# A two-layer diffusion step on one core: the passage to the second layer, the router and the weight units of the expert loop reordered

## The reference

```python
def _swiglu(h, wg, wu, wd):
    return (jax.nn.silu(h @ wg) * (h @ wu)) @ wd

def _moe(h, w_router, wg, wu, wd):
    ...
    logits = (t @ w_router).astype(jnp.float32)
    top_v, top_i = lax.top_k(logits, TOP_K)
    top_w = jax.nn.softmax(top_v, -1)
    ...
    for e in range(N_EXPERTS):
        y = y + gates[:, e:e + 1] * _swiglu(t, wg[e], wu[e], wd[e])

def _layer(x, cond, lp, ffn, latent, ctx_k, ctx_v, s0):
    mod = jax.nn.silu(cond) @ lp['w_mod'] + lp['b_mod']
    sh1, sc1, g1, sh2, sc2, g2 = jnp.split(mod[:, None, :], 6, -1)
    h = x * (1 + sc1) + sh1
    mix, kb, vb, s = _mixer(h, lp, latent, ctx_k, ctx_v, s0)
    x = _ln(DN_ALPHA * x + g1 * mix, lp['ln_g'][0], lp['ln_b'][0])
    h = x * (1 + sc2) + sh2
    x = _ln(DN_ALPHA * x + g2 * ffn(h), lp['ln_g'][1], lp['ln_b'][1])
```

## Time and profile before

| | us |
|---|---|
| median of 3 runs | 1976.18 (1976.16 to 1976.51) |
| the profiled execution | 1976.08, of which the span is 1973.8 |
| PE busy | 1883.9 (95%) |
| DVE busy | 1401.5 (71%) |
| ACT busy | 1088.6 (55%) |
| last down matmul of the dense stage ends, about | 566.5 |
| first matmul of cva in layer 1 | 608.76 |
| gather for the first expert begins | 932.14 |
| one pass of the expert loop | 125.32 |

### The profile page before, as it was taken

One profiled execution on the slowest core, in us unless ns is written; L12 is line 12 of the kernel. 1 busy time (PEld: TensorE's weight loads), 2 busy tenths in 40 slices (PEclk: granted clock), 3 DMA queues, 4 the chain that ended last, 5 costly groups with the idle time before them and its releaser, 6 DMA issues.

```text
span 1973.8 us, 23686 instructions
## 1 busy us (share of the span) xinstructions
PE 1883.9 (95%) x9097; PEld 1416.1 (72%) x9097; DVE 1401.5 (71%) x1424; ACT 1088.6 (55%) x1025; POOL 29.8 (2%) x53
## 2 busy tenths in 40 slices
PE   4999999999979999998999999999999999999995
PEld 2885554677858855545788888888888888888884
DVE  2576853644564858525788888988889888888886
ACT  2443332444434533313777767777777777777773
POOL 1000010000000000100000000000000000000000
PEclk9999999999989999998999999999999999999997
DMA  9765344576573553434799999999999999999993
GB/s 353 254 228 205 128 157 147 196 255 213 193 262 140 201 213 139 136 126 150 272 367 341 354 337 358 364 341 356 354 341 363 342 357 362 333 366 341 352 368 110
DMA packets 228430, 531.69 MB, mean 269 GB/s; under 512 B 5128, under 2 KB 7744, under 8 KB 228368
## 3 DMA queue, kind: packets, MB, share of 16 engines
q1 hardware_dynamic: 161728, 369.77, 52.2%
q10 hardware_dynamic: 63472, 151.27, 21.0%
q0 software_dynamic: 3168, 9.80, 1.6%
HBM read 528.20 MB, written 2.62 MB: 269 GB/s over the span
## 4 chain that ended last, share of the span: by engine, by line
PE 94%; DVE 2%; ACT 2%; issue 1%; DMA 1%; ACTq 0%; POOL 0%; DVEq 0%; POOLq 0%
PE ps L856 20%; PE ps L857 20%; PE ps L858 20%; PE ps L786 16%; PE ps L843 2%; PE ps L807 2%; PE ps L809 2%; PE ps L810 2%; PE ps L1240 2%; PE ps L820 2%; PE ps L1268 1%; PE ps L1118 1%; DMA arena<-in_cv_w 1%; PE ps L971 0%; PE ps L1002 0%
## 5 line engine op out<-in xcount | busy, mean ns | idle before, releaser
L2274 DVE TENSOR_TENSOR arena_r<-ring,arena_r 128x2048 fp32r<-128x2048 f32 x224 | 512.0, 2292 | 107.8 <-ACT arena_r L1410 103.4
L1410 ACT ACTIVATE arena_r<-ring 128x2048 fp32r<-128x2048 f32 x224 | 428.9, 1915 | 85.1 <-PE ps L858 85.0
L856 PE MATMUL ps<-arena_r 128*128 128x512 f32 x1128 | 449.3, 398 | 24.2 <-DVE arena_r L1776 14.5
L857 PE MATMUL ps<-arena_r 128*128 128x512 f32 x1128 | 443.2, 393 | 0.0
L858 PE MATMUL ps<-arena_r 128*128 128x512 f32 x1128 | 413.0, 392 | 0.0
L2274 DVE TENSOR_TENSOR ring_r<-ring,ring_r 128x2048 fp32r<-128x2048 f32 x113 | 258.9, 2291 | 37.5 <-ACT ring_r L1410 35.9
L856 PEld LDWEIGHTS ps<-arena_r 128*128 128x128 f32 x1128 | 214.4, 190 | 71.5 <-issue 20.1
L858 PEld LDWEIGHTS ps<-arena_r 128*128 128x128 f32 x1128 | 214.2, 190 | 46.4
L857 PEld LDWEIGHTS ps<-arena_r 128*128 128x128 f32 x1128 | 214.6, 190 | 44.0
L1410 ACT ACTIVATE ring_r<-ring 128x2048 fp32r<-128x2048 f32 x113 | 216.7, 1917 | 50.0 <-PE ps L858 49.8
L856 PE MATMUL ps<-ring_r,arena_r 128*128 128x512 f32 (+1 forms) x592 | 235.2, 397 | 0.7 <-issue 0.7
(11 more groups left out here) (236 smaller groups left out, 1918.6 us busy)
## 6 DMA issues: line engine op xcount, KB each, us to landing
ring<-in_moe_w_gate SPq DMA_DIRECT2D x57, 2048.0 KB, 7.8
ring<-in_moe_w_up ACTq DMA_DIRECT2D x48, 2048.0 KB, 7.8
ring<-in_moe_w_down SPq DMA_DIRECT2D x32, 2048.0 KB, 7.8
ring<-in_w_in SPq DMA_DIRECT2D x28, 2048.0 KB, 8.4
ring<-in_w_mod SPq DMA_DIRECT2D x24, 2048.0 KB, 8.6
ring<-in_moe_w_down ACTq DMA_DIRECT2D x24, 2048.0 KB, 7.8
ring<-in_moe_w_up SPq DMA_DIRECT2D x8, 2048.0 KB, 7.9
ring<-in_ffd_w_gate SPq DMA_DIRECT2D x5, 2048.0 KB, 13.9
```

What stands on the lines that cost most here:

```text
L856: mm(o_, hi, w_hi[:, n], start=start, stop=False)
L857: mm(o_, hi, w_lo[:, n], start=False, stop=False)
L1410: act_(e_part(j)[0], raw_part(j), ACT.Copy).then_inc(part_hi, 1)
L2274: V.tensor_tensor(w_lo, raw_part(j), w_hi.bitcast(F32), ALU.subtract).then_inc(part_lo, 1)
```

## The change

Four things are done at once.

1. **Passage.** Layer 1's modulations 4 and 5 move from the passage into layer 1's mixer, where layer 0 has them; the turning of modulation 3 moves into the dense stage. The last four down parts (from `DAPART` = 18) run first for group 0 and then for group 1. All four weight parts of layer 1's v are cast before the norms, two of them in buffers of their own, and the modulation's columns are gathered before them as well. PE turns x of both groups before v; ACT modulates both halves of group 0. The slots of the ring shift by one from there on.
2. **Mixers.** The turnings of `kbtok` and `kctxT` stand before the gate matmul `mgate(5, 1)`, and ACT's copies before the silu. Modulation 11 stands before the wait for mT.
3. **Router.** ACT's exponential stands before the last two gate copies and the first cast, and the casts of parts 0 and 1 both stand before the loop; in the loop ACT runs one part further ahead.
4. **Expert loop.** A gate and up unit now holds 512 rows of 512 gate columns and 512 up columns; G and U of one width are summed up over four parts, side by side in two banks. Every unit is loaded by two transfers of 1 MB, all from SP's queue. The turning of the width before stands after the second of the four parts, the scattering after the first two parts of the pass, and the bank table is new.

PE's order in the passage, before: the end of the down matmuls (L856 to L858 with `ring_r`), modulation (L843 with `condT`), turnings (L820; `x` is the normalised x, `arena` a modulation row).

The diff, cut to its core:

```diff
-        if l:
-            modT(l, 3), mod(l, 4)
         for g in range(G):
             p("hT", l, g, 0), p("hT", l, g, 1)
-            if l and g == 0:
-                modT(l, 4), mod(l, 5), modT(l, 5)
+        for g in range(G):
             p("v", l, g)
...
+DAPART = FF_D // P - 4
...
-EUNITS = []
-for _i in range(EC):
-    EUNITS += [("g", _i), ("u", _i)]
+EUNITS = [("gu", _i, _h) for _i in range(EC) for _h in range(2)]
...
+            if phase_of(j) == "mixer1":
+                b = (20992, 18432, 0, 2048)[s] if j - PHASE["mixer1"] < DPARTS else (15360, 17408, 0, 2048)[s]
+            else:
+                b = (0, 2048, 15360, 17408)[s]
...
+                halves = [(dst[:, :, 512 * h:512 * h + 512],
+                           a[w][0, e, rows_, 512 * name[1]:512 * name[1] + 512].rearrange("(c p) n -> p c n", p=P))
+                          for h, w in enumerate(("moe_w_gate", "moe_w_up"))]
             eng.wait_ge(part_lo, E * EQ + (PART_BASE + 2 * (i - XRING + 1)))
-            dst = slot(i % XRING).rearrange("p (c n) -> p c n", c=4 if name[0] == "d" else 8)
-            eng.dma_start(dst, e_source(name, e)).then_inc(w_loaded[i % XRING], 16)
+            for to, src in halves:
+                eng.dma_start(to, src).then_inc(w_loaded[i % XRING], 16)
...
+                turned(("kbtok", l), [kbT[:, j * T:j * T + P] for j in range(4)])
+                pe.wait_ge(ctx_in, 16 * (l + 1))
+                turned(("kctxT", l), [kctx[:, j * P:(j + 1) * P] for j in range(4)])
                 mgate(5, 1)
...
+                mod_mm(l, 11)
                 for g in range(G):
                     copied("mT", l, g, 0), copied("mT", l, g, 1)
-                mod_mm(l, 11)
...
+                    for g in range(G):
+                        for f in range(DAPART, FF_D // P):
+                            dense_down(f, [g])
...
+                        gu = [(e_claim(p, E, "G", i), 0), (e_claim(p, E, "U", i), 512)]
+                        for q in range(4):
...
+                                inss = split_mm([(o_, slice(D * c + n, D * c + n + 512)) for o_, n in gu], hg_hi[:, ks], hg_lo[:, ks],
+                                                w_hi, w_lo, k == 0, k == KD - 1)
...
+                            if q == 1 and i:
+                                turn(i - 1)
...
+                    st.next(gate_arg)
+                    act_(route[:, 100:102], route[:, 98:100], ACT.Exp).then_inc(gate_exp, 1)
+                gate_row(1)
...
+                    v1 = DFIRST["v", 1]
+                    early_hi(v1), early_hi(v1 + 1)
+                    act_(stat[:, 54:55], ident[:, 0:1], ACT.Sqrt)
+                    early_hi(v1 + 2)
                     norm_sqrt(1)
+                    early_hi(v1 + 3)
                 else:
-                    expert_high(0, 0, 0)
-                    st.next(gate_arg)
-                    act_(route[:, 100:102], route[:, 98:100], ACT.Exp).then_inc(gate_exp, 1)
+                    expert_high(0, 0, 0), expert_high(0, 0, 1)
...
-                    for j in range(1, EQ + 1):
-                        if (j + 3) % 2 == 0 and (j + 3) // 2 in ACT_UNITS:
-                            load_expert_unit(sc, E, e, (j + 3) // 2)
+                    for j in range(2, EQ + 2):
...
+                    early_lo(DFIRST["v", 1]), early_lo(DFIRST["v", 1] + 1)
+                    mod_columns(0, 4, 8, 1, modT[:, 96:192].rearrange("p (c g) -> p c g", g=G), 64)
                     dv.wait_ge(ln_in, 32 * 2)
```

More of the change, by code:

```diff
@@ L193, in plan @@
         p("oT", l, 1)
+        p("kbtok", l), p("kctxT", l)
         mg(l, 5, 1)
         p("cvT", l, 0), p("cvT", l, 1)
-        p("kbtok", l), p("kctxT", l), p("bias", l, 0), p("bias", l, 1)
+        p("bias", l, 0), p("bias", l, 1)
         for i in range(4):
@@ L351 @@
             EUSED.append(USED_PER)
-ACT_UNITS = range(EPARTS, len(EUNITS), 2)
 HI_PER = 4 + EC
@@ L1073, in _ @@
                     turned(("cvT", l, g), [acc[:, g * 512 + j * P:g * 512 + (j + 1) * P] for j in range(4)])
-                turned(("kbtok", l), [kbT[:, j * T:j * T + P] for j in range(4)])
-                pe.wait_ge(ctx_in, 16 * (l + 1))
-                turned(("kctxT", l), [kctx[:, j * P:(j + 1) * P] for j in range(4)])
                 pe.wait_ge(bias_in, 64 * (l + 1))
@@ L1415, in _, with modulated @@
             for l in range(DEPTH):
-                def modulated(kind, sh, scl, g):
-                    await_product(sc, kind, l, g, 1)
-                    for j in range(4):
-                        k = 4 + j
-                        ins = act_(hT[:, k * T + g * P:k * T + (g + 1) * P], bank((kind, l, g, 1))[:, j * P:(j + 1) * P],
-                                   ACT.Identity, bias=modcol(l, sh + k, g), scale=modcol(l, scl + k, g))
-                    free(ins, kind, l, g, 1)
+                def modulated(kind, sh, scl, g, halves=(1,)):
+                    for h in halves:
+                        await_product(sc, kind, l, g, h)
+                        for j in range(4):
+                            k = 4 * h + j
+                            ins = act_(hT[:, k * T + g * P:k * T + (g + 1) * P], bank((kind, l, g, h))[:, j * P:(j + 1) * P],
+                                       ACT.Identity, bias=modcol(l, sh + k, g), scale=modcol(l, scl + k, g))
+                        free(ins, kind, l, g, h)
                 def norm_sqrt(n):
@@ L1442, in _ @@
                 else:
[L1443 to L1447 removed]
+                    modulated("hT", 0, 8, 0, range(2))
+                    high_h("hT", l, 0)
+                    norm_sqrt(1)
+                    modulated("hT", 0, 8, 1)
+                    high_h("hT", l, 1)
                 hi_unit("cva")
@@ L1551, in _ @@
                 gla_turned(1)
+                take(kbtok, ("kbtok", l))
+                take(kctxT, ("kctxT", l))
                 mgate(5, 1)
@@ L1561, in _ @@
                     free(ins, "cvT", l, g)
-                take(kbtok, ("kbtok", l))
-                take(kctxT, ("kctxT", l))
                 softmax_exp(Pm)
```

220 lines of the change are left out of this document (97 added, 123 removed).

## The result

The changed kernel takes 1942.04 us (median of 4 runs, 1941.47 to 1942.18), the kernel before 1976.17; the ratio is 0.9822, 95% interval 0.9811 to 0.9834. The profiled execution took 1941.47 us with a span of 1939.2, against 1976.08 and 1973.8: 34.6 us less. The forecast was 1944, range 1937 to 1953.

The account below looks back on a forecast made before the run. PE, on the chain of waits for 94% of the span, was taken as the bound, so gains lie at seams where it waits. Passage -11.9, keys -8.0, modulation 11 -3.8, router -8.5 sum to -32.2: 1976.1 to 1943.9, say 1944, range 1937 to 1953.

Parts of the forecast that it names:

- passage with modulation 3's turning: Dense stage to layer 1's cva: 42.2 us shrinks to 24.8, -17.4; modulation 3's turning moved to the dense stage, +0.5.
- modulations 4 and 5 in layer 1's mixer: Layer 1's mixer, cva to rope: taking these modulations lengthens it from 75.33 to layer 0's 80.35 us, +5.0.
- turning of cached keys, twice: Before attention scores in each mixer: copies ahead of silu remove PE's 2.41 us idle, 9.48 to 4.0 us; -8.0 together.
- modulation 11, twice: Each mixer: its eight matmuls fill PE's 1.92 us wait for ACT's copies of mT; -3.8 together.
- router, parts 0 and 1, loop: Router and first expert: exponential 3.4 us earlier, part 1 cast during the gather, -8.5 (bounds -9.5 and -4); loop 0.
- last link: Passage: low part of h, on DVE after group 1's norm, ends at 11.1 us; v of group 0 starts about 11.75.
- nine of v's matmuls at half clock: Passage, v of group 0: 9 of 24 matmuls at 0.427 us and 15 at 0.233, together 7.3 us.
- the rule of the Trainium skill: Passage: transposes do not count as work for the clock, so v stays slow about four more matmuls, 0.8 us; not counted.
- A: Expert loop: loads become the bound; gain gone at 0.19 us over per unit, 1991 us at 6.25 us; chance 0.08.
- B: Expert loop: ACT or DVE late at parts 4 and 8, PE waits twice an expert, 5 to 8 us; chance 0.12.
- C: Passage yields half: v of group 0 waits for something placed too early, -6 instead of -11.9, 1950 us; chance 0.08.
- D: Router not earlier: parts 0 and 1 at half clock or table load on gate copies, -4, 1948 us; chance 0.05.

## Why the prediction was right

| term | forecast | measured |
|---|---|---|
| passage with modulation 3's turning | -16.9 | -18.0 |
| modulations 4 and 5 in layer 1's mixer | +5.0 | +4.9 |
| turning of cached keys, twice | -8.0 | -8.5 |
| modulation 11, twice | -3.8 | -3.6 |
| router, parts 0 and 1, loop | -8.5 | -9.9 |
| start of the kernel | 0 | +0.5 |
| sum | -32.2 | -34.6 |

The passage, the keys, the mixer and the router gave more than forecast, modulation 11 and the start a little less: the forecast of 1944 was 2 us too high.

**Passage.** The chain was right in its first links: group 0's norm under the down matmuls, then DVE's norm of group 1 with PE idle for 6.40 us. Its last link was another one. The sum lets v wait for the low part of h and adds 0.65 us for which it names no row; it leaves out PE's turning of x of group 1, which stands ahead of v. In the trace that turning took 1.62 us at half clock and ended 0.41 us after the low part. Counted from 561.46, as from 566.5 there, the low part ended at 10.7 (forecast 11.1), v started at 11.1 (11.75) and v of both groups took 12.7 us (13.0). The 1.1 us are these: DVE's chain 0.4, the way from its end to v's start 0.25, v 0.35. That v's start came out so near is in part luck: the unnamed 0.65 us stood where the missing link took 0.41.

I took nine of v's matmuls at half clock. The 5.5 us read from the earlier trace rows hold 13 of them at 0.427, and the trace has 8. Five traces with this passage unaltered have 2 to 8, and v took 11.55 to 12.68 us in them, so this term is known to a microsecond at best. By the rule of the Trainium skill that the prediction quotes (TensorE: Matmul & The Clock Gate, Part 4: PE-mode transpose) there would have been about four more than nine. None of the five traces shows that, though each has the turning right ahead of v and the idle time of 6.40 us ahead of the turning.

**Keys, modulation 11, the mixer's +5.0.** Each came out within 0.3 us a place, because each was read from a stretch that either exists elsewhere in the trace without the wait, or has one wait in it. One condition was misread: the cached keys are not loaded long before. In the changed kernel they land at 258.41 in layer 0 and their turning starts at 260.00; in layer 1 it is 783.40 and 786.56. No wait arose, but the margin was 1.6 and 3.2 us.

**Router.** The exponential gave the forecast 3.4. Two steps failed, with opposite signs. I had part 0 follow the gather as before; but G and U are now filled side by side, so the first matmul claims both banks that the gather's halves lie in, and waits until both halves are copied: 1.7 us of idle. That is read from the program and the releaser in the trace; no run with other banks tests it. Against that, the gather ran 0.9 us faster at a higher clock, part 2 followed ST at once where my sum of times had left a microsecond, and 1.1 us came from the clock ahead of the router, in code that the change doesn't touch. Seven of the eight traces that hold the whole change have this 1.1 us, and the one with eight transfers a unit has not, so what brings it is not shown. Parts 0 and 1 ran at full clock, as I had taken.

**Loop.** 0 forecast, +0.04 an expert measured. My slack was near: 0.3 and 0.5 us estimated at parts 4 and 8, 0.55 and 0.62 in the trace, the tightest is part 6 with 0.50; the extra ACT work shows that it is slack.

**Rivals.** A is out at 1 MB and at 512 KB; by the rule of 341 GB/s (the Trainium skill, DMA: Bandwidth & Descriptors, Bandwidth) the loop would have been 30 us longer; the page measured that with transfers issued from GpSimd. The loop here ran at 351 GB/s with transfers of 1 MB and 352 with 512 KB. B did not come about, but anything over half a microsecond more of ACT work at part 4 brings it. C: v of group 0 did wait for something that I had not placed, the turning of x of group 1, but it cost less than the 0.65 us that I had added, and v was slow for 3.6 us only. D: part 1 had no wait and no half clock.

## What to carry to other kernels

Price each seam by the chain of the engine that releases it, and look for a stretch of the same trace that already does the work without the wait: the terms read so came out within 0.3 us a place, while the passage, added up as a chain with a link missing, was 1.1 us off. Work that the critical engine must do anyway belongs into the idle time of a seam rather than out of it; the change moved two modulations from the passage to a full stage, and putting them into the waits that remained won that back. Where two products begin side by side, as G and U here, their first instruction waits for the later of both banks: look at what last held them.

## What the hardware showed that I had not expected

The clock's return after an idle time differs between executions and between kernels at unchanged code. Behind the same idle time of 6.40 us and the same turning, 2 to 8 of v's matmuls ran at half clock in five traces, and v took 11.55 to 12.68 us. It made 1.1 us of difference in the stretch ahead of the router, and 1.2 us behind a wait of 2 us, where the clock read 0.84 in one trace and 1.00 in another. Terms of about a microsecond can't be told from it by one trace.

A loop body with eight transfers a unit made SP issue the load of unit 1 3.8 to 4.6 us late in six of eight passes, those begun by the jump back, where four or two transfers a unit had at most 0.5 us. The transfers themselves, at a quarter of the size, moved the same 350 GB/s.
